# Reordering four seams of a two-layer decoder trunk: where a norm total, low parts, a root and Sqrt tables stand

## The reference

```python
def shared_kv(x, kv_norm_g, w_k, w_v, k_norm_g):
    h = rmsnorm(x, kv_norm_g)
    k = rmsnorm((h @ w_k).reshape(Bn, S, DIFF_HEADS, 2, DIFF_HEAD), k_norm_g)
    v = (h @ w_v).reshape(Bn, S, DIFF_HEADS, 2 * DIFF_HEAD)
    ...
def diff_attention(h, k, v, rel_bias, w_q, q_norm_g, lam, subln_g, w_o, layer_idx):
    q = rmsnorm((h @ w_q).reshape(Bn, S, H, 2, d), q_norm_g)
    ...
        logits = jnp.einsum('bhcqd,bhckd->bhcqk', q_blk, k).astype(jnp.float32) * scale
        logits = logits + bias[None, :, None]
        logits = jnp.where(rel >= 0, logits, -jnp.inf)
        probs = jax.nn.softmax(logits, axis=-1)
        attn = probs[:, :, 0] - lam_full * probs[:, :, 1]
        return jnp.einsum('bhqk,bhkv->bhqv', attn.astype(v.dtype), v)
    ...
    o = rmsnorm(o, subln_g) * (1 - lambda_init)
    return o.reshape(Bn, S, H * 2 * d) @ w_o
```

## Time and profile before

| | us |
|---|---|
| runs | 1680.52, 4015.96, 1686.51 |
| median of these | 1686.51 |
| the profiled execution | 1681.86 |
| its span in the trace | 1680.0 |
| PE busy in the span | 1569.5 |
| mean granted clock of PE | 0.977 |

### The profile page before, as it was taken

How to read it: one execution, slowest core, us unless ns; L and a number is a source line. 1 busy time by engine, 2 the same in 40 slices (tenths; PEclk the granted TensorE clock), 3 DMA queues, 4 the chain that set the end, 5 groups by cost and what they waited for, 6 DMA issues and landing times. The chain is left out here.

```text
span 1680.0 us, 20542 instructions
## 1 busy us (share of the span) xinstructions
PE 1569.5 (93%) x7335; PEld 1253.7 (75%) x7335; DVE 778.9 (46%) x1233; ACT 635.6 (38%) x1007; POOL 666.1 (40%) x427
## 2 busy tenths in 40 slices
PE   4699997999999999999999799989899999999998
PEld 3565776989568788888887578756487888888876
DVE  4875959775464430023125764567544310232133
ACT  4654453555433221122234332356533221222242
POOL 4323343555314344444443444342133444444442
PEclk8899998999999999999999999999999999999999
DMA  4122200011102323323323133220013333233331
GB/s 135 50 76 76 75 26 1 1 55 63 51 23 78 100 100 100 113 76 99 101 100 108 62 115 101 75 75 1 1 51 100 100 101 112 75 100 100 100 100 50
DMA packets 123525, 127.18 MB, mean 76 GB/s; under 512 B 8316, under 2 KB 120060, under 8 KB 123448
## 3 DMA queue, kind: packets, MB, share of 16 engines
q1 hardware_dynamic: 122720, 124.90, 22.8%
q0 software_dynamic: 352, 0.66, 0.2%
q10 hardware_dynamic: 376, 0.61, 0.1%
HBM read 124.03 MB, written 2.12 MB: 75 GB/s over the span
## 5 line engine op out<-in xcount | busy, mean ns | idle before, releaser
L440 POOL TENSOR_TENSOR wlo<-wraw,whi 128x1024 fp32r<-128x1024 f32 x108 | 260.9, 2416 | 806.2 <-ACT whi L1236 757.5
L600 PE MATMUL pb<-xh,whi 128*128 128x512 f32 x1184 | 476.5, 402 | 28.1 <-DVE xl L1762 15.8
L601 PE MATMUL pb<-xl,whi 128*128 128x512 f32 x1184 | 465.2, 393 | 0.0
L602 PE MATMUL pb<-xh,wlo 128*128 128x512 f32 x1184 | 464.9, 393 | 0.0
L600 PEld LDWEIGHTS pb<-xh,whi 128*128 128x128 f32 x1184 | 224.7, 190 | 102.9 <-issue 41.7
L1236 ACT ACTIVATE whi<-wraw 128x2048 fp32r<-128x2048 f32 (+1 forms) x111 | 209.1, 1884 | 223.1 <-PE pb L602 223.1
L443 POOL TENSOR_TENSOR wlo<-wraw,whi 128x1024 fp32r<-128x1024 f32 x111 | 274.4, 2472 | 20.9 <-ACT whi L1236 20.9
L601 PEld LDWEIGHTS pb<-xl,whi 128*128 128x128 f32 x1184 | 225.1, 190 | 48.0 <-issue 3.4
L602 PEld LDWEIGHTS pb<-xh,wlo 128*128 128x128 f32 x1184 | 224.8, 190 | 47.9
L600 PE MATMUL pb<-hid_h,whi 128*128 128x512 f32 x512 | 199.3, 389 | 0.0
L601 PE MATMUL pb<-hid_l,whi 128*128 128x512 f32 x512 | 199.2, 389 | 0.0
(11 more groups left out here) (281 smaller groups left out, 1945.7 us busy)
## 6 DMA issues: line engine op xcount, KB each, us to landing
wraw<-in_mlp_w_dram SPq DMA_DIRECT2D x128, 512.0 KB, 4.3
wraw<-in_rwkv_w_rkvo_dram SPq DMA_DIRECT2D x32, 512.0 KB, 4.3
wraw<-in_ple_w_gate_dram SPq DMA_DIRECT2D x16, 512.0 KB, 3.9
xtok<-in_x_dram SPq DMA_DIRECT2D x8, 512.0 KB, 5.8
wraw<-in_w_k_shared_dram SPq DMA_DIRECT2D x8, 512.0 KB, 4.0
wraw<-in_w_v_shared_dram SPq DMA_DIRECT2D x8, 512.0 KB, 4.3
wraw<-in_diff_w_q_dram SPq DMA_DIRECT2D x8, 512.0 KB, 4.0
wraw<-in_diff_w_o_dram SPq DMA_DIRECT2D x8, 512.0 KB, 4.0
```

The source lines that it names most:

```text
L440: pool.tensor_tensor(wlo[:, par, front], wraw[:, par, front], whi[:, par, front].bitcast(F32), ALU.subtract)
L600: mm(o, wh, ah, start=first, stop=False)
L601: mm(o, wh, al, start=False, stop=False)
L602: return mm(o, wl, ah, start=False, stop=last)
```

## The change

At the shared key: PE's norm total moves from step 7 of key block 0 to step 3 of key block 1. qk_total(0) moves from step 5 of block 1 to step 1 of block 2, which keeps qk_total(2) at its step 5. ACT makes the high part of each weight block one block ahead of before and at the head of each turn, before roots and squares. DVE multiplies a block with rstd before it normalises the heads of the pair before.

At the queries: ACT and DVE make five of the eight xh and xl tiles of the query input during value block 3, DVE ahead of that block's multiply, ACT ahead of the copies of value tiles 4 and 5; the other three stay behind.

At attention's start: ACT's root for the last four query heads stands ahead of high(N_DO + 1) and of all exponentials. It was between the second and the third pair of them.

Tables: `root_table(i)` is a Sqrt of one element into an unused word. It stands before the recurrence loop, behind the last Sigmoids of the first layer, and behind the attention loop ahead of head_take(7).

```diff
--- before.py
+++ after.py
@@ -1120,7 +1120,7 @@
             for b in range(4):
                 pe.wait_ge(s.dense_v, 72 + 2 * (b - 1))
                 dense_block(N_KS + b, b % 2, b % 2, 2, X_KV if b == 0 else None,
-                            {5: qk_total(2 * b - 2)} if b else {7: lambda: norm_total(4)})
+                            (None, {3: lambda: norm_total(4)}, {1: qk_total(0), 5: qk_total(2)}, {5: qk_total(4)})[b])
             for b in range(4):
                 pe.wait_ge(s.dense_v, 80 + 2 * (b - 1))
                 dense_block(N_VS + b, b % 2, b % 2, 2, None, {5: v_turn(2 * b - 2)} if b else {5: qk_total(6)})
@@ -1243,6 +1243,10 @@
                     A(xh[:, k, :], src, ACT.Copy).then_inc(s.x_hi, 1)
                 else:
                     A(xh[:, k, :], src, ACT.Copy, scale=gain).then_inc(s.x_hi, 1)
+
+            def root_table(i):
+
+                A(small[0:1, 88 + i:89 + i], eps_n[0:1, :], ACT.Sqrt)
 
             def norm_root(i):
                 act.wait_ge(s.norm_ps, i)
@@ -1481,6 +1485,7 @@
                 if q == HALF + 5:
                     turned(0, 1)
             turned(0, 2)
+            root_table(0)
             for k in range(NQ + 1):
                 if k:
                     take_u(1, k - 1)
@@ -1600,6 +1605,8 @@
                         act.wait_ge(s.dense_v, 64 + 88 * layer + c + 1)
                         A(tmp[:, m, :], tmp[:, m, :], ACT.Sigmoid).then_inc(s.sig, 1)
                     if layer == 0 and b == 3:
+                        root_table(1)
+                    if layer == 0 and b == 3:
                         act.wait_ge(s.upd, 8)
                         splits(V_KV, 8 * (n + 4), 6)
                     if n + 3 + b < N_ALL:
@@ -1637,23 +1644,26 @@
                 A(VT[:, i, :, :].rearrange("p t v -> p (t v)"), pb[6 + i % 2][:, :], ACT.Copy).then_inc(s.v_ev, 1)
 
             for b in range(4):
+                if b < 3:
+                    high(N_KS + b + 2, b % 2)
                 if b == 0:
                     norm_root(3)
                 else:
-                    high(N_KS + b + 1, (b + 1) % 2)
                     head_root(2 * b - 2)
                     head_root(2 * b - 1)
                 head_square(2 * b)
                 head_square(2 * b + 1)
             for b in range(4):
                 high(N_VS + b + 1, (b + 1) % 2)
+                if b == 3:
+                    splits(V_N10, 8 * (N_VS + 3), 0, 5)
                 if b:
                     v_copy(2 * b - 2)
                     v_copy(2 * b - 1)
                 else:
                     head_root(6)
                     head_root(7)
-            splits(V_N10, 8 * (N_VS + 3))
+            splits(V_N10, 8 * (N_VS + 3), 5)
             for b in range(4):
                 high(N_Q + b + 1, (b + 1) % 2)
                 if b == 0:
@@ -1694,17 +1704,17 @@
                     act.wait_ge(s.o_ps, h - 1)
                 A(tmp[:, h % 2, :], pb[5 + h % 2][:, :], ACT.Square).then_inc(s.o_sq, 1)
 
+            act.wait_ge(s.qk_ps, 16)
+            A(rstd[:, :], pb[6][:, :], ACT.Sqrt, bias=eps_n, scale=1.0 / HD).then_inc(s.qk_rt, 1)
             high(N_DO + 1, 1)
             for i in range(1, 32 + 4):
                 if i - 1 < 32:
                     exps(i - 1)
-                if i == 2:
-                    act.wait_ge(s.qk_ps, 16)
-                    A(rstd[:, :], pb[6][:, :], ACT.Sqrt, bias=eps_n, scale=1.0 / HD).then_inc(s.qk_rt, 1)
                 if 0 <= i - 3 < 32:
                     attn_copy(i - 3)
                 if i >= 8 and i % 4 == 0:
                     head_take((i - 8) // 4)
+            root_table(2)
             head_take(7)
             act.wait_ge(s.o_ps, 8)
             act.wait_ge(s.rows_0, 2)
@@ -2234,20 +2244,22 @@
                     tt(dsts[m], pb[2 * (b % 2) + m][:, :], rstd[:, :], ALU.mult).then_inc(sem, 1)
 
             for b in range(4):
+                times_rstd(N_KS + b, b, [KT[:, 2 * b + m, :] for m in range(2)])
                 if b:
                     head_norm(2 * b - 2)
                     head_norm(2 * b - 1)
-                times_rstd(N_KS + b, b, [KT[:, 2 * b + m, :] for m in range(2)])
             for b in range(4):
                 if b == 0:
                     head_norm(6)
                     head_norm(7)
                 else:
+                    if b == 3:
+                        splits(V_N10, X_Q, 0, 5)
                     dve.wait_ge(s.v_tr, 2 * b)
                 dve.wait_ge(s.pe_step, 8 * (N_VS + b + 1))
                 for m in range(2):
                     tt(tmp[:, 2 + m, :], pb[2 * (b % 2) + m][:, :], rstd[:, :], ALU.mult).then_inc(s.dense_v, 1)
-            splits(V_N10, X_Q)
+            splits(V_N10, X_Q, 5)
             for b in range(4):
                 if b == 0:
                     dve.wait_ge(s.v_tr, 8)
```

## The result

| | before | changed |
|---|---|---|
| median, us | 1682.77 (11 runs: 1680.52 to 1686.51, and one of 4015.96) | 1690.71 (11 runs, 1688.87 to 1693.26) |
| ratio, 95% interval | | 1.0050 [1.0042, 1.0058] |
| profiled execution, its span | 1681.86, 1680.0 | 1690.04, 1688.2 |
| mean granted clock of PE | 0.977 | 0.975 |

The changed kernel is half a per cent slower; 1689.2 was forecast. The page's part 1 shows no engine with more work: PE is busy 1572.9 us for 1569.5, the difference being matmuls at half clock. The rest of the 8.2 us of span is time in which PE stands.

The account below looks back on a forecast made before the run. PE is busy 93%, so reordering pays only where PE stands or its clock falls. -5.0 + 15.0 - 3.9 + 2.4 - 1.3 + 0.1 = +7.3 us on 1681.86 gives 1689.2; range 1681 to 1700.

Parts of the forecast that it names:

- Seam 1: Shared-key norm total a block later: PE's 5.88 us wait becomes 4.2 us ahead of the second key block; minus 5.0 us.
- Key heads: Third and fourth key and first value block: totals outrun the serial root, scaling and square chain; plus 15.0 us.
- Seam 2: First query block: early low parts of the query input remove a 2.2 us wait and 1.7 of slow clock; minus 3.9.
- Group norm: Sqrt table load ahead of the group-norm root moves into an earlier ACT wait; minus 1.3 us.
- Head of attention: Attention's start: the root ahead of high(N_DO+1) delays GpSimd's low part, first scaling and combinations; plus 2.4 us.
- The rival that ACT sets the pace there: Attention's start is bound by ACT, so saved table loads count: minus 2.6 for plus 2.4, 1684 us; 10%.
- End: End of attention loop: new Sqrt load and tiny activation end about 0.3 us behind ACT's wait; plus 0.1 us.
- The head chain keeps up: Rival: key-head squares come in time, +0.8 in place of +15.0, net -6.9, 1675 us; 10%.
- Lateness runs on: Rival: key-head lateness continues into the second to fourth value blocks; 1695 to 1700 us, 9% shared with full clock loss.
- the full 2.9 us for each new pause: Rival: each new PE pause draws the full 2.9 us of clock loss; 1695 to 1700, 9% shared with lateness running on.
- the clock never returns: Rival: PE's clock stays down between pauses, 38 us of key-head-stretch matmuls take twice as long; 1723 us, 1%.

Follow-up runs that it names:

- the second execution: The changed kernel executed and profiled once more with no edit, to see how much stage lengths differ between executions: 1689.76 us.

## Why the prediction was right, and where it was off

**Seam 1, -5.0, measured -4.9.** Right in each step: KS1 starts behind GpSimd's low part, 3.85 us late for 4.2 forecast, the total waits for nothing, and KS1 takes 13.5 us where 10.8 + 1.0 + 1.7 were forecast.

**Key heads, +15.0, measured +15.3.** The mechanism held: the run without doubled totals takes all of the loss away, the one with the old queue order most of it. By block, forecast and measured: KS2 18.0 and 17.4, KS3 18.8 and 19.9, VS0 17.3 and 17.1. The pauses were forecast at 2.5, then 1.0 and 3.4, then 2.6, and are 2.77, 1.46 and 2.92, and 2.54. What was off is the clock: I gave it 0.9 in KS2 and 1.7 in KS3. Less the pauses, and less 14.5 and 12.65 us of matmuls, the profiled execution leaves 0.1 and 2.9 for it, the second execution 1.8 and 3.4. The second one's key heads cost +17.5, as in the run of this seam alone. So two of these three executions lie 2.5 us above the forecast, and that the first is within 0.3 of it is luck in where the clock fell.

**Seam 2, -3.9, measured -4.0.** Right, wait and clock both. The first five xl tiles took DVE 7.17 us beside GpSimd, more than the 5.5 I had allowed, and DVE still had the room. But alone it moved the runs by 2.7, so not all of a stage's gain reaches the end.

**Group norm, -1.3, measured -0.8.** This step failed. I took the whole load as exposed. The load ran from 464.35 to 465.63, but the root needs PE's variance total, which the timeline has at 462.94 for 1.89, to 464.83; half a microsecond of the load lay beside it. In the changed kernel ACT waits 1.59 us for that total ahead of its root. I had made just this subtraction for the end of the attention loop and not here. The Trainium skill, "ScalarE: Activation LUTs", section "What ACT_TABLE_LOAD costs", would have had 2.7 here, an estimate from its load of 1.28 and its drain of 1.38; the trace bears out neither that nor its drain: in the changed kernel the load at 1121.95 lasts 1.28 and the exponential behind it starts at 1123.24.

**Head of attention, +2.4, measured +3.4.** POOL's first scaling came 2.3 us later relative to the last total, as forecast and as the run with the root first repeats. The further 1.1 is clock, in and between the windows of 0.57 and 0.89; the second execution, at 1.00 in the later one, has +2.0 for the stage. The rival that ACT sets the pace there is out: with the loads gone and the high part in place, the ratio is 1.0004 [0.9995, 1.0013].

**End, +0.1, measured -0.2.** The root waits 1.12 us for PE's total, the load is hidden. (In the prediction the load of before "ran 2 us"; the row shows 1.28, and the sum didn't use the 2.) Behind it there are 0.7 us that I had at nothing, clock by the windows (0.57 over 1214 to 1222, and 0.62 in the second execution, which has none of the 0.7).

**Rivals.** "The head chain keeps up" is out for the change as made, by 9.7 us of waits at L1087. With the totals spaced out it comes true, and that kernel ran at 1677, near the 1675 worked out for the rival. "Lateness runs on" is out: the v_turns stand 11.8 us apart. So is the full 2.9 us for each new pause: the three in KS2 and KS3 drew 3.0 us of clock together in one execution and 5.2 in the other. That the clock never returns is out too: it is at 1.00 in Q0.

**The sum, +7.3; measured +7.9 by the medians, +8.2 by the spans.** It is nearer than its parts. The stages from the group norm on come to +9.5 in both executions of the changed kernel; what brings the spans back is a front 1.4 and 1.8 us shorter than in the profile of before. No term of the forecast stood for the front, and over the 13 profiles its end lies anywhere from 461.1 to 463.3. That part of the agreement is luck.

**Base.** I took the profiled execution's 1681.86 over the median 1686.51 of three runs. The later medians of before, 1681.87 to 1683.22, bear that out. From the other base the same sum would have given 1693.8, over 3 us too high.

## What to carry to other kernels

When a total is moved later, follow what reuses its buffer. Here a square could not be made until the head two in front had been scaled, so two totals in one block, with the queues behind them turned round, cost 15 to 17 us where the moved total gained 5; the same shift of every total by one whole block costs no wait and keeps 4.5 of the 5. A copy that another engine's long work hangs on (here GpSimd's low part, and PE behind it) belongs ahead of a wait in its queue, not behind one: `high()` behind a root cost 2.3 us at the attention loop, and ahead of a residual's wait it gained 3.9 (by the runs; 3.2 by the trace). Before a table load is counted as a gain, look up when the operand of its function arrives.

## What the runs showed of the hardware

**The clock behind a pause is not a function of the pause.** PE's pause of 2.08 us at KS0's start comes in every profile with the same work around it. In both profiles of before and the second of the changed kernel the clock stayed at 1.00; in the first of the changed kernel it was 0.57 over 944 to 948 and the matmul behind the pause took 0.70 us for 0.47. Over all 13 profiles it stayed up through KS0 in eight and fell within 1 us of the pause's end in five. The fall cost nothing here: KS0 took 16.62 us with it in the first execution of the changed kernel and 16.61 without it in the second, since KS1 waits for GpSimd's low part in either case. In the prediction I had read from one execution that a pause of this length does not slow the clock, which does not hold. Nor did the second profile of the changed kernel slow down where the first did. One profile's slow stretch need not be a property of the kernel; what moves it between executions was not tried. The Trainium skill, "TensorE: Matmul & The Clock Gate", Part 1, says that what watches PE's activity is free-running and does not restart with the kernel, so that the same kernel can meet it at another phase; the two executions of the changed kernel agree with that. Those of before have their slow stretches at the same places, 0.4 us apart like their pauses, and tell nothing either way.

**A stage with two lengths.** From the first L841 at the start of the recurrence (291.02 in before) to the last variance total, a stretch that no edit touches, 13 profiles have either 170.4 to 170.7 us (five) or 171.8 to 172.1 (eight), the two executions of the changed kernel one each. Differences of 1.5 us between two profiles can come from there. This too goes with the clock. Windows of before (long) and of the second execution of the changed kernel (short):

```profile
297.00:305.00 8.00, 7.37 (x36) 7.37 (x37) 4.48 (x15) 2.39 (x7) 0.81 (x3) 0.57 0.00 0
...
297.00:305.00 8.00, 7.56 (x50) 7.45 (x51) 5.27 (x16) 3.21 (x10) 1.56 (x3) 0.79 0.00 0
```

Over the whole stage, its length times the missing share of the clock is 3.8 to 4.1 us in the five short ones and 5.1 to 5.5 in the eight long ones, and the lengths follow these numbers from profile to profile to within 0.1 us. Why the clock comes out one way or the other stays open.

**DVE beside GpSimd.** A scaling of a head takes 0.75 us alone and 1.48 while GpSimd subtracts (998.16); two xl tiles 1.41 and 4.80. Moving GpSimd's work into a gap of PE can so land on DVE's path.
